# Item 0's tokens by a one-hot product, and layer 0's results summed and normed on token rows

## Chip, cores and metric

One NeuronCore of a Trainium2 chip. The metric is the device time of one execution in microseconds (us). Engines in the profile: PE (TensorE; PEld are its weight loads), DVE (VectorE), ACT (ScalarE), POOL (GpSimd), SP (SyncE, which here only issues transfers). "The granted clock" is the share of TensorE's full clock that the throttle allowed: 1.00 is 2.4 GHz, 0.50 is 1.2 GHz.

## The reference, cut to what matters

288 token rows of width 1024 (256 of a prompt, 8 x 4 of a sample group) pass two layers: a gated chunk MLP and a block-sparse attention, each followed by a mixture of 16 experts.

```python
hp = hp + mixer(rms_norm(hp, norm1[i]))           # i = 0: chunk gating, i = 1: QKV, attention, w_o
hp = hp + hier_moe(rms_norm(hp, norm2[i]), ...)   # the same for the sample rows hs

def hier_moe(h, ...):                             # x: token rows
    g_w, g_idx = top_k(softmax(x @ w_group + b_group), 1)
    e_w, e_idx = top_k(softmax((x @ w_router + b_router)[group g_idx]), 2)
    gates = one_hot(expert, 16) weighted by e_w / sum(e_w) * g_w
    hid = silu(x @ w_gate[e]) * (x @ w_up[e]) * gates[:, e]
    y = sum over e of hid @ w_down[e]
```

All arithmetic on the path of the result is fp32.

## The kernel before

All weights and the cache pages stream from DRAM once. Token rows are worked in three chunks, `tok`: two of 128 rows and one of 32 (the sample). The residual stream lies transposed in `xT` (128 partitions x 8 x 288), the normed input of a product in `hT`. Each engine has one instruction list, in order, and semaphores join them; there is no scheduler, so a wait holds back everything after it on its engine. SP issues nearly all weight transfers, from one queue in program order.

*Into the experts* (`project`, `route`). While the mixer's last product is added to `xT`, PE transposes `xT` back to token rows, six half rows in PSUM banks 0, 1, 2, 3, 4 and 6 (`ROW_ORDER`). ACT squares them, and copies them scaled by the reciprocal root to `tokbuf` and on to DRAM (`h_rows`). DVE ranks the router's logits and gives each token's two choices a slot number, 64 slots to an item (item q < 16 is expert q; experts that get more than 64 tokens have more items at the end).

*Items* (`experts`). For item q, DVE compares each token's slots with 128 lane numbers (`one_hot`, six instructions: three chunks, two choices), PE multiplies the result by `marks` (`table_of`) and DVE sums this to row indices (`indices`). From item 2 on the same table also gives the gate of each slot; items 0 and 1 get theirs in a step of their own (`weigh`, `first_gates`). POOL gathers the 64 token rows, as 128 half rows, from `h_rows`; PE transposes them (`rows_up`, reading columns at a step of four), DVE multiplies by the norm's gain (`x_tile`), PE forms gate and up (`gate_up`), ACT and DVE the gated product, PE transposes it (`gated_up`) and multiplies by the down weights (`down`), ACT copies the result out and POOL scatters it to DRAM (`y_rows`, two results for each token).

The order on PE is: tables 0 and 1, some products that only keep it busy (`idle_products`; in layer 1 the 24 transposes of `rows`, which form token rows of `xT` again for the last sum), gates of items 0 and 1, table 2, `rows_up(0)`, and then for each q: `gate_up(q)`, `gated_up(q-1)`, `table_of(q+3)`, `rows_up(q+1)`, `down(q-1)`.

Expert weights (3 MB an item) go round five buffers: items 0 to 3 are loaded ahead, item 4 (`expert_own`) goes to space that is free only after routing (its down weights to `tokbuf`), and from item 5 on the gate and up weights wait for `gate_up(q-5)`, the down weights for `down(q-5)`.

*Out of layer 0.* SP loads each token's first results into `tokbuf`, ACT the second into `y_second`, chunk by chunk. DVE adds the two, PE transposes to banks 0 to 7, DVE adds to `xT`, ACT squares, PE sums by a product with `mean_d`, ACT takes the root, DVE the reciprocal over 128 x 288 and scales into `hT` (`norm(3)`). Then come 16 QKV tiles of eight products, each tile followed by what normalises and rotates the heads before it. The QKV weights are four quarters of 2 MB.

*Out of layer 1.* The same loads; DVE adds the two results and then the raw rows `x_rows`, chunks in the order 0, 1, sample, and SP stores each.

The lines of the deleted last loop of layer 0 on DVE, and of item 0's start on PE, are in the diff below.

## Time and profile before

| | |
|---|---|
| median of 3 runs | 715.23 us (709.33 to 717.9) |
| the profiled execution | 717.95 us, span 716.1 us |
| mean granted TensorE clock | 0.929 |
| busy: PE, weight loads, DVE, ACT, POOL | 87%, 60%, 38%, 19%, 17% of the span |
| read from DRAM, written | 178.96 MB, 13.50 MB; 269 GB/s over the span |

The profile is of one execution. Busy shares are means over stages with different limits; times in timelines are from the span's start, and a merged row gives the start of its first instruction and the time to the end of its last.

### The profile page before, as it was taken

How to read it: one execution, taken by the hardware profiler on the slowest of the kernel's cores; microseconds unless marked ns; L12 is line 12 of the kernel's file. 1: busy time of each engine (PE TensorE's matmuls, PEld its weight loads, DVE VectorE, ACT ScalarE, POOL GpSimd, SP SyncE). 2: the span in 40 equal slices, each digit the busy share in tenths (PEclk: the TensorE clock that was granted, in tenths of full speed). 3: DMA queues.
4: the chain of work that ended last, by engine and by line, in shares of the span. 5: the costliest groups of instructions: out<-in, count | busy, mean ns of one | idle time of the engine just before them, and what ended most of it. 6: DMA issues, size and time to landing. Idle time of an engine off the chain costs nothing. (4 is left out here: it accounts for less than half of the span.)

```text
span 716.1 us, 11289 instructions
## 1 busy us (share of the span) xinstructions
PE 625.4 (87%) x4125; PEld 427.5 (60%) x4125; DVE 271.6 (38%) x821; ACT 135.2 (19%) x304; POOL 119.1 (17%) x175
## 2 busy tenths in 40 slices
PE   3999999968999988789999997985996899998860
PEld 1777787855655554567667674674785655555430
DVE  2221231144544422435775776340015363442224
ACT  4112001050111111111111454221015211111100
POOL 0000000002232321004222321230000123222110
PEclk9998999977999999789999998998997899999975
DMA  9886004066899993899423765689906789999525
GB/s 342 271 350 234 2 0 184 1 242 239 336 411 409 410 410 158 281 387 339 124 74 111 241 230 185 229 307 392 413 15 247 284 315 411 412 411 413 203 102 199
DMA packets 60980, 184.83 MB, mean 258 GB/s; under 512 B 12244, under 2 KB 12934, under 8 KB 56702
## 3 DMA queue, kind: packets, MB, share of 16 engines
q1 hardware_dynamic: 49022, 153.16, 56.4%
q0 software_dynamic: 10560, 26.24, 10.3%
q10 hardware_dynamic: 1344, 4.72, 1.7%
q8 instruction: 33, 0.54, 0.3%
q14 instruction: 21, 0.17, 0.1%
HBM read 178.96 MB, written 13.50 MB: 269 GB/s over the span
## 5 line engine op out<-in xcount | busy, mean ns | idle before, releaser
L1293 PE MATMUL PS<-hT,half_b 128*128 128x288 f32 x384 | 105.7, 432 | 7.6 <-DMA half_b<-in_b_w_o 4.3
L1293 PEld LDWEIGHTS PS<-hT,half_b 128*128 128x128 f32 x384 | 75.8, 202 | 31.5 <-issue 9.1
L547 POOL DMA_INDIRECT zT<-h_rows,where x35 | 36.2, 1036 | 256.1 <-DMA h_rows<-tokbuf 214.9
L1293 PE MATMUL PS<-hT,half_a 128*128 128x288 f32 x256 | 68.5, 422 | 0.0
L1399 PE MATMUL PS<-ew_in,zT 128*64 128x256 f32 x480 | 58.9, 401 | 4.7 <-DMA ew_in<-in_moe_w_up 3.0
L552 POOL DMA_INDIRECT y_rows<-zT,where x33 | 33.5, 1015 | 159.0 <-ACT zT L708 154.0
L1293 PEld LDWEIGHTS PS<-hT,half_a 128*128 128x128 f32 x256 | 48.7, 195 | 17.7 <-DVE zT L1141 2.8
L1399 PEld LDWEIGHTS PS<-ew_in,zT 128*64 128x64 f32 x480 | 37.9, 146 | 28.4 <-issue 15.9
L1017 DVE COPY zT<-PS 128x128 f32<-128x128 f32 x33 | 9.6, 292 | 110.6 <-PE PS L1410 104.9
L947 DVE TENSOR_SCALAR zT<-lanes,slots 128x128 bf16<-128x128 bf16 (+1 forms) x222 | 39.0, 248 | 2.5 <-DVE slots L1048 1.6
L708 ACT COPY zT<-PS 128x512 f32<-128x512 f32 x33 | 19.3, 586 | 99.5 <-PE PS L1421 99.5
L701 ACT ACTIVATE zT<-PS 64x256 f32<-64x256 f32 x33 | 12.5, 377 | 132.5 <-PE PS L1399 132.5
L857 DVE TENSOR_TENSOR xT<-PS,xT 128x288 f32<-128x288 f32 x16 | 7.3, 458 | 73.9 <-PE PS L1293 73.9
L1005 DVE TENSOR_TENSOR zT<-PS,gains_rows 128x512 f32<-128x512 f32 x35 | 24.2, 691 | 23.0 <-PE PS L1388 22.0
L1293 PE MATMUL PS<-zT,half_a 128*128 128x288 f32 x128 | 32.9, 410 | 0.0
L1421 PE MATMUL PS<-ew_down,zT 128*64 128x512 f32 x120 | 31.4, 647 | 1.3 <-issue 1.3
L1388 PE MATMUL PS<-cst,zT 128*128 128x128 f32 x140 | 27.4, 321 | 2.3 <-DMA zT<-h_rows,where 2.3
L1399 PE MATMUL PS<-sq,zT 128*64 128x256 f32 x96 | 23.5, 401 | 4.5 <-DMA hT<-in_moe_w_up 4.5
L1293 PEld LDWEIGHTS PS<-zT,half_a 128*128 128x128 f32 x128 | 23.7, 190 | 6.1
L1388 PEld LDWEIGHTS PS<-cst,zT 128*128 128x128 f32 x140 | 20.4, 211 | 8.6 <-issue 4.5
L1279 PE MATMUL PS<-cst 128*128 128x288 f32 x64 | 23.9, 538 | 0.0
L1399 PE MATMUL PS<-hT,zT 128*64 128x256 f32 x96 | 23.5, 401 | 0.0
(303 smaller groups left out, 896.0 us busy)
## 6 DMA issues: line engine op xcount, KB each, us to landing
ew_in<-in_moe_w_gate SPq DMA_DIRECT2D x15, 1024.0 KB, 16.2
ew_in<-in_moe_w_up SPq DMA_DIRECT2D x15, 1024.0 KB, 17.9
ew_down<-in_moe_w_down SPq DMA_DIRECT2D x15, 1024.0 KB, 15.8
half_b<-in_moe_w_gate SPq DMA_DIRECT2D x6, 1024.0 KB, 12.9
half_b<-in_moe_w_up SPq DMA_DIRECT2D x6, 1024.0 KB, 15.6
half_b<-in_moe_w_down SPq DMA_DIRECT2D x6, 1024.0 KB, 11.8
half_a<-in_moe_w_gate SPq DMA_DIRECT2D x6, 1024.0 KB, 11.2
half_a<-in_moe_w_up SPq DMA_DIRECT2D x6, 1024.0 KB, 12.8
```

What stands on the lines that cost most here:

```text
L547: pool.indirect_dma_start(out=x_slots[:, u, :], out_offset=None, in_=h_dram.rearrange("t (h n) -> (t h) n", h=2), in_offset=bass.IndirectO ...
L552: pool.indirect_dma_start(out=y_dram[l].rearrange("t k (h n) -> (t k h) n", h=2), out_offset=bass.IndirectOffsetOnAxis(ap=where[:, r, 1:2] ...
L701: act.activation(silu, PS[0:SLOT, 2 + u_of(q), 0:EF], ACT.Silu).then_inc(el["silued"], 1)
L708: act.copy(y_slots[:, u, :], PS[:, 5 + u, :]).then_inc(el["y_sb"], 1)
L947: last = dve.tensor_scalar(hot_of(q)[0:m, c, k, :], lanes[0:m, :], slots[0:m, c, k:k + 1], -float(SLOT * q) if isinstance(q, int) else 0.0 ...
L1005: dve.tensor_tensor(x_slotsT[:, u].rearrange("p j h n -> p (j h) n"), PS[:, u, :].rearrange("p (m n) -> p m n", n=SLOT), gains_rows[:, l, ...
L1017: dve.tensor_copy(hidT, PS[:, 4, 0:FB * SLOT].rearrange("p (f n) -> p f n", f=FB)).then_inc(el["ht_sb"], 1)
L1279: pe.matmul(PS[:, bank, 0:T], ident, cst[:, 0:T], start=True, stop=True)
L1293: mm = pe.matmul(PS[:, bank, 0:T], w[:, k, col:col + P], src[:, k, :], start=(k == 0), stop=(k == KT - 1))
L1388: mm = pe.transpose(PS[:, u, j * P:(j + 1) * P], x_slots[:, u, bass.ds(j, P, 4)], ident)
L1399: mm = pe.matmul(PS[f * SLOT:(f + 1) * SLOT, 2 + u, 0:EF], x_slotsT[:, u, k % 4, k // 4, :], w_in[f][:, k, :], start=(k == 0), stop=(k == ...
L1421: mm = pe.matmul(PS[half * SLOT:(half + 1) * SLOT, 5 + u, :], hidT[:, f, :], w_down[:, f, half * HALF:(half + 1) * HALF], start=(f == 0), ...
```

## The change

Item 0 is no longer gathered. `tokbuf` holds the scaled token rows when they go to DRAM; DVE makes a 0/1 matrix of tokens by the 64 slots of item 0 (`first_hot`), and PE multiplies `tokbuf` (as the weights, columns at a step of four) by it, which gives item 0's tokens transposed in bank 0. For this, in both layers, ACT first copies the six raw half rows from PSUM to `x_rows` (`raw_rows`); in layer 1 this replaces the 24 transposes of `rows`. Table 1 now comes first; table 0, the gates and table 2 come behind `gate_up(0)`. The own expert's down weights wait for the product.

Layer 0's results are summed on token rows with the raw rows, the sample chunk first (`BACK_ORDER`), normed there (ACT's square with a row sum, root, DVE's reciprocal and scaling), and then transposed straight into `hT`. The raw sums are transposed into `xT` between the first four QKV tiles. The second and fourth quarter of the QKV weights are loaded when the sums are done, since the raw rows lie in their space. Layer 1's last sums and stores also take the sample first.

The diff, cut to its core:

```diff
+        hot_first = z_flat[:, 2048:2048 + NT * SLOT].rearrange("p (c n) -> p c n", c=NT)
...
-        Y_ORDER = [KT - 1] + list(range(KT - 1))
+        BACK_ORDER = (CH,) + tuple(range(CH))
...
+                sp.wait_ge(E[l]["xt"], 1)
                 expert_down(l, BUFS - 1, w_down, s_down)
...
-                for c, (at, m) in enumerate(tok):
+                for c in BACK_ORDER:
+                    at, m = tok[c]
...
-            for u in range(4):
+            for u in (0, 2, 1, 3):
+                if u == 1:
+                    sp.wait_ge(S["yt"], NT)
                 load(w_qkv_at[u], w_qkv[:, :, u * HALF:(u + 1) * HALF], s_home[QKV_HOME[u]][0])
...
-                for q in range(2):
-                    pool.wait_ge(E[l]["idx"], 2 * q + 2)
-                    gather(q, q, q)
+                pool.wait_ge(E[l]["idx"], 2)
+                gather(1, 1, 1)
...
+            def raw_rows():
+                for row, half, bank in ROW_ORDER:
+                    n = tok[row][1]
+                    act.copy(x_rows[row][0:n, half * HALF:(half + 1) * HALF], PS[0:n, bank, :]).then_inc(S["xrows_sb"], 1)
...
             route(0)
+            raw_rows()
             experts(0)
-            squares(3)
-            root(3)
-            for i in range(LH + 1):
-                if i < LH:
-                    act.wait_ge(S["qkv_sb"], i + 1)
-                    if i >= KT:
-                        act.wait_ge(S["hms"], i - KT + 1)
-                    act.activation(sq[:, i % KT, :], zT[:, i, :], ACT.Square).then_inc(S["hsq"], 1)
-                if i >= 1:
-                    h = i - 1
-                    act.wait_ge(S["hms"], h + 1)
-                    if h >= 2:
-                        act.wait_ge(S["hrec"], h - 1)
-                    act.activation(std[:, h % 2, :], PS[:, 4 + h % 2, 0:T], ACT.Sqrt, bias=eps[:, :]).then_inc(S["hroot"], 1)
+            ready_for(ACT.Sqrt)
+            for i, c in enumerate(BACK_ORDER):
+                n = tok[c][1]
+                act.wait_ge(S["yt"], i + 1)
+                act.activation(y_squares[0:n, c, :], tokbuf[0:n, c, :], ACT.Square, accum_out=y_sums[0:n, c:c + 1]).then_inc(S["squared"], (3, 3, 2)[i])
+                act.wait_ge(S["squared"], 3 * KT + (3, 6, 8)[i])
+                act.activation(y_std[0:n, c:c + 1], y_sums[0:n, c:c + 1], ACT.Sqrt, bias=eps[0:n, :], scale=1.0 / D).then_inc(S["rooted"], 1)
+            for k in range(KT):
+                act.wait_ge(S["xr_t"], KT + k + 1)
+                act.copy(xT[:, k, :], PS[:, 6 + k % 2, 0:T]).then_inc(S["xr_sb"], 1)
+                if k % 2 == 1:
+                    head_squares(k // 2)
...
+            def first_hot(l):
+                chain.link(dve.scalar_tensor_tensor(out=slot_first[:, :], in0=gates[:, :, 0], scalar=1.0, in1=chosen_any[:, :, 0],
+                                                    op0=ALU.add, op1=ALU.mult))
+                for c, (_, m) in enumerate(tok):
+                    last = dve.tensor_scalar(hot_first[0:m, c, :], lanes[0:m, 0:SLOT], slot_first[0:m, c:c + 1], -1.0,
+                                             ALU.subtract, ALU.is_equal)
+                last.then_inc(S["dispatch"], 1)
...
-                for q in range(2):
-                    one_hot(l, q)
-                    indices(l, q, q)
+                one_hot(l, 1)
+                first_hot(l)
+                indices(l, 1, 1)
                 weigh(l)
+                x_tile(0, 0)
+                one_hot(l, 0)
+                indices(l, 0, 0)
                 first_gates(l)
                 one_hot(l, 2)
                 indices(l, 2, 2)
                 one_hot(l, 3)
...
-            for c, (_, m) in enumerate(tok):
+            def back_sum(i):
+                c, m = BACK_ORDER[i], tok[BACK_ORDER[i]][1]
                 dve.wait_ge(s_yb[c], 2 * 16)
-                dve.tensor_tensor(tokbuf[0:m, c, :], tokbuf[0:m, c, :], y_second[0:m, c, :], ALU.add).then_inc(S["yt"], 1)
-            for i, k in enumerate(Y_ORDER):
-                dve.wait_ge(S["hrows_t"], i + 1)
-                dve.tensor_tensor(xT[:, k, :], PS[:, k, 0:T], xT[:, k, :], ALU.add).then_inc(S["added"], 1)
-            dve.wait_ge(S["added"], KT)
-            norm(3)
+                chain.link(dve.tensor_tensor(tokbuf[0:m, c, :], tokbuf[0:m, c, :], y_second[0:m, c, :], ALU.add))
+                if i == 0:
+                    dve.wait_ge(S["xrows_sb"], 2 * NT)
+                dve.tensor_tensor(tokbuf[0:m, c, :], tokbuf[0:m, c, :], x_rows[c][0:m, :], ALU.add).then_inc(S["yt"], 1)
+            def back_scale(i):
+                c, m = BACK_ORDER[i], tok[BACK_ORDER[i]][1]
+                dve.wait_ge(S["rooted"], 3 + i + 1)
+                dve.wait_ge(S["yt"], i + 1)
+                chain.link(dve.reciprocal(y_rec[0:m, c:c + 1], y_std[0:m, c:c + 1]))
+                dve.tensor_scalar(y_second[0:m, c, :], tokbuf[0:m, c, :], y_rec[0:m, c:c + 1], None, ALU.mult).then_inc(S["x_row"], 1)
+            back_sum(0)
+            back_sum(1)
+            back_scale(0)
+            back_sum(2)
+            back_scale(1)
+            back_scale(2)
+            for k in range(KT):
+                col = KT + k
+                dve.wait_ge(S["hrows_t"], k + 1)
+                dve.tensor_scalar(hT[:, k, :], PS[:, k, 0:T], gains[:, col:col + 1], None, ALU.mult).then_inc(S["normed"], 1)
...
-                for q in range(2):
-                    table_of(q)
-                if l == 1:
-                    pe.wait_ge(S["hrows_sb"], 4 * NT)
-                    rows(xT, "xrows", "xrows_sb", 0)
-                else:
-                    idle_products(4, 5)
-                first_gates()
-                table_of(2)
-                idle_products(3, 5)
-                if l == 1:
-                    pe.wait_ge(S["xrows_sb"], 2 * NT)
-                else:
-                    pe.wait_ge(S["hrows_sb"], 2 * NT)
-                rows_up(0, gathered(0)[1], 0)
+                table_of(1)
+                pe.wait_ge(S["dispatch"], l + 1)
+                pe.wait_ge(S["hrows_sb"], 2 * NT * (l + 1))
+                pe.wait_ge(S["xrows_sb"], 2 * NT * (l + 1))
+                for j in range(4):
+                    for h in range(2):
+                        for c, (_, m) in enumerate(tok):
+                            mm = pe.matmul(PS[:, 0, (2 * j + h) * SLOT:(2 * j + h + 1) * SLOT], tokbuf[0:m, c, bass.ds(h * HALF + j, P, 4)],
+                                           hot_first[0:m, c, :], start=(c == 0), stop=(c == CH))
+                mm.then_inc(el["xt"], 1)
                 for q in range(LAST):
                     gate_up(q, *tiles_in(q), q - 1)
                     if q >= 1:
                         gated_up(q - 1)
+                    else:
+                        table_of(0)
+                        first_gates()
+                        table_of(2)
                     if q + 3 <= LAST + 1:
                         table_of(q + 3)
                     rows_up(q + 1, gathered(q + 1)[1], q)
...
-            for c, (at, n) in enumerate(tok):
-                pe.wait_ge(S["yt"], c + 1)
-                for k in Y_ORDER:
-                    mm = pe.transpose(PS[:, k, at:at + n], tokbuf[0:n, c, k * P:(k + 1) * P], ident[0:n, 0:n])
-                    if c == CH:
+            for i, c in enumerate(BACK_ORDER):
+                at, n = tok[c]
+                pe.wait_ge(S["x_row"], NT + i + 1)
+                for k in range(KT):
+                    mm = pe.transpose(PS[:, k, at:at + n], y_second[0:n, c, k * P:(k + 1) * P], ident[0:n, 0:n])
+                    if i == NT - 1:
                         mm.then_inc(S["hrows_t"], 1)
-            mean_squares(3)
...
+                if i < KT // 2:
+                    for k in (2 * i, 2 * i + 1):
+                        if k >= 2:
+                            pe.wait_ge(S["xr_sb"], KT + k - 1)
+                        for c, (at, n) in enumerate(tok):
+                            mm = pe.transpose(PS[:, 6 + k % 2, at:at + n], tokbuf[0:n, c, k * P:(k + 1) * P], ident[0:n, 0:n])
+                        mm.then_inc(S["xr_t"], 1)
+                if i == KT // 2 - 1:
+                    pe.wait_ge(S["xr_sb"], 2 * KT)
```

## Rows read from the trace of the kernel before

**Rows 1.** The page: busy time by engine, and shares of the chain that ended last.

```profile
PE 625.4 (87%) x4125; PEld 427.5 (60%) x4125; DVE 271.6 (38%) x821; ACT 135.2 (19%) x304; POOL 119.1 (17%) x175
...
PE 10%; DMA 9%; DVE 2%; issue 1%; POOL 0%; ACT 0%; SPq 0%; POOLq 0%; DVEq 0%; ACTq 0%
```

**Rows 2.** Windows of 20 us, experts of layer 0; columns as in the first line.

```profile
core 0: us, PE busy (x) PEld busy (x) DVE busy (x) ACT busy (x) POOL busy (x), PEclk, DMA share, GB/s
200.00:220.00 20.00, 20.00 (x158) 11.73 (x156) 8.01 (x33) 2.89 (x6) 6.05 (x7) 1.00 1.03 410
...
260.00:280.00 20.00, 17.43 (x128) 9.81 (x124) 4.76 (x17) 2.69 (x6) 4.93 (x6) 1.00 0.79 317
```

**Rows 3.** Timeline, entrance to layer 0's experts: start, us, engine, line, operation.

```profile
157.22 0.24 ACT L680 ACTIVATE ex<-ex 128x60 f32<-128x60 f32 x1
...
161.37 1.23 POOL L547 DMA_INDIRECT zT<-h_rows,where  x1 [140.33 <-DMA h_rows<-tokbuf]
...
170.30 5.25 PE L1399 MATMUL PS<-ew_in,zT 128*64 128x256 f32 x32 [0.87 <-DVE zT L1005]
...
177.42 3.67 PE L1399 MATMUL PS<-half_a,zT 128*64 128x256 f32 x32 [0.88 <-DVE zT L1005]
...
184.39 0.34 SPq L378 DMA_DIRECT2D ew_down<-in_moe_w_down  x1
```

**Rows 4.** The same timeline: gates, one_hot(2), table 2, one_hot(3).

```profile
163.40 0.69 PE L1378 MATMUL PS<-marks,zT 128*128 128x3 bf16 x12
...
164.33 1.05 DVE L947 TENSOR_SCALAR zT<-lanes,slots 128x128 bf16<-128x128 bf16 x6
...
165.44 0.39 PE L1367 MATMUL PS<-marks,zT 128*128 128x9 bf16 x6 [1.35 <-DVE zT L947]
...
166.15 1.05 DVE L947 TENSOR_SCALAR zT<-lanes,slots 128x128 bf16<-128x128 bf16 x6
```

**Rows 5.** Timeline, entrance to layer 1's experts.

```profile
549.51 0.24 ACT L680 ACTIVATE ex<-ex 128x60 f32<-128x60 f32 x1
...
551.81 4.77 PE L1352 MATMUL PS<-cst,xT 128*128 128x128 f32 x24
...
552.97 0.59 ACT L687 COPY half_a<-PS 128x512 f32<-128x512 f32 x1 [3.22 <-PE PS L1352]
...
563.36 3.67 PE L1399 MATMUL PS<-ew_in,zT 128*64 128x256 f32 x32 [0.87 <-DVE zT L1005]
...
568.92 3.67 PE L1399 MATMUL PS<-half_a,zT 128*64 128x256 f32 x32 [0.88 <-DVE zT L1005]
```

**Rows 6.** Timeline of PE alone: products with one moving column.

```profile
64.27 4.82 PE L1484 MATMUL PS<-mean_d,sq 128*128 128x1 f32 x48
```

**Rows 7.** Weight loads of two lines: durations in ns, min/median/max.

```profile
L1388 PEld LDWEIGHTS PS<-cst,zT x140: 195/212/231, 168.3 to 695.7; 128*128 128x128 f32 x140
...
L1312 PEld LDWEIGHTS PS<-cst,xT x48: 96/140/144, 132.2 to 540.7; 128*128 128x128 f32 x32, 128*32 128x32 f32 x16
```

**Rows 8.** Windows of 1 us, columns as in rows 2.

```profile
166.00:167.00 1.00, 1.00 (x5) 0.70 (x5) 0.97 (x8) 0.00 (x0) 0.00 (x0) 0.85 1.02 418
...
173.00:174.00 1.00, 1.00 (x10) 0.71 (x8) 0.00 (x0) 0.00 (x0) 0.00 (x0) 0.74 0.00 0
```

**Rows 9.** Timeline, layer 0's results to the first QKV tile.

```profile
294.67 1.23 DVE L1131 TENSOR_TENSOR tokbuf<-tokbuf,zT 128x1024 f32<-128x1024 f32 x1 [4.69 <-DMA zT<-y_rows]
...
297.96 2.35 DVE L1131 TENSOR_TENSOR tokbuf<-tokbuf,zT 128x1024 f32<-128x1024 f32 x2 [2.06 <-DMA zT<-y_rows]
...
312.14 9.69 PE L1293 MATMUL PS<-hT,half_b 128*128 128x288 f32 x32 [3.29 <-DVE hT L850]
```

**Rows 10.** Timelines of ACT, DVE and PE: row square, row scaling, three transposes.

```profile
8.62 1.04 ACT L735 ACTIVATE zT<-tokbuf 32x1024 f32<-32x1024 f32 x1
...
10.54 1.40 DVE L1078 TENSOR_SCALAR zT<-tokbuf,rec 128x1024 f32<-128x1024 f32 x2
...
43.69 0.56 PE L1526 MATMUL PS<-cst,tokbuf 128*128 128x128 f32 x3
```

**Rows 11.** Timeline, layer 1's last sums.

```profile
708.87 1.22 DVE L1270 TENSOR_TENSOR tokbuf<-tokbuf,zT 128x1024 f32<-128x1024 f32 x1 [1.20 <-DMA tokbuf<-y_rows]
```

More of the change, by code:

```diff
@@ L306, in gathered, with turn_of @@
         def gathered(q):
-            return f"in{q % 2}", 16 * (q // 2 + 1)
+            return f"in{q % 2}", 16 * ((q + 1) // 2)
+        def turn_of(q):
+            return 1 - q if isinstance(q, int) and q < 2 else q
         def scattered(q):
@@ L680, in route @@
                 act.activation(ex[:, :, :], ex[:, :, :], ACT.Exp).then_inc(S["exped"], 1)
-            def rows(src_sem, base, dst, done):
-                for i in range(2 * NT):
-                    _, n = tok[i // 2]
-                    act.wait_ge(S[src_sem], base + i + 1)
-                    act.copy(dst[i // 2][0:n, (i % 2) * HALF:(i % 2 + 1) * HALF], PS[0:n, i % 4, :]).then_inc(S[done], 1)
+            def raw_rows():
+                for row, half, bank in ROW_ORDER:
+                    n = tok[row][1]
+                    act.copy(x_rows[row][0:n, half * HALF:(half + 1) * HALF], PS[0:n, bank, :]).then_inc(S["xrows_sb"], 1)
             def experts(l):
@@ L836, in _ @@
             route(1)
-            rows("xrows", 0, x_rows, "xrows_sb")
+            raw_rows()
             experts(1)
@@ L1263, in _ @@
             past_rows(1)
+            dve.wait_ge(S["xr_sb"], 2 * KT)
             project(KT)
@@ L1343, in route @@
                 idle_products(3, 5)
-            def rows(src, s, taken, base):
-                for i in range(2 * NT):
-                    at, n = tok[i // 2]
-                    if i >= 4:
-                        pe.wait_ge(S[taken], base + i - 3)
-                    for j in range(4):
-                        mm = pe.transpose(PS[0:n, i % 4, j * P:(j + 1) * P], src[:, (i % 2) * 4 + j, at:at + n], ident)
-                    mm.then_inc(S[s], 1)
             def experts(l):
```

50 lines of the change are left out of this document (33 added, 17 removed).

## Prediction, made before the change was run

> **What bounds the kernel now.** Read the page first: TensorE (PE) is busy for 87% of a 716.1 us span, and the chain that ended last is made of PE and DMA pieces in nearly equal parts [rows 1]. So a saving counts only where PE or a transfer stands still for it, and the next view must be one by stage. The 20 us windows show the expert stage: PE busy 20.00 of 20 while the DMA engines are at 1.03 of their share, 410 GB/s, until a stretch before 280 in which PE has waits again [rows 2]. PE and weight transfers are in step through the stage, and a delay at its entrance is handed on to its exit. The reason is SP's queue: the down weights of item 5 are issued at 184.39, when item 0's down product has ended, and all later weights stand behind them [rows 3]. From there the transfers are back to back. Whatever moves 184.39 moves the end of the stage.
>
> Third view: the timeline of the entrance to layer 0's experts. ACT finishes the exponent at 157.46; the gather of item 0 starts at 161.37, when the rows written to DRAM have landed; item 0's gate/up product starts at 170.30 and takes 5.25 us (item 1's takes 3.67), item 1's starts at 177.42 [rows 3]. Between the two lies a gap of only 1.9 us (170.30 + 5.25 to 177.42) for one table, four transposes and their scaling. Layer 1 has the same shape: exponent done at 549.75, product 0 at 563.36, product 1 at 568.92 [rows 5]. Last, the two tails: layer 0's from the landed results to the first QKV tile, 297.96 to 312.14 [rows 9], and layer 1's from its second landed chunk, 708.87, on [rows 11].
>
> **Part 1, item 0 by a product (both layers).** Removed: one gather and four transposes in each layer, and in layer 1 the 24 transposes of the raw rows, 4.77 us of PE [rows 5]. Added in front of product 0: four small vector instructions (DVE is through them before ACT is, so nothing on the path), six ACT copies, and the product itself. The copies are a new wait: the product waits for all six raw row halves, and behind it in PE's queue is the whole expert stage. In layer 0 ACT starts them at 157.46; the copy of a 128x512 bank takes 0.59 us [rows 5], six take 3.5, so PE may begin at 161.0. In layer 1: 549.75 + 3.5 = 553.25.
>
> The product is 24 fp32 matmuls, recorded as 48 instructions, each with a 128-column weight load and 64 moving columns. Nothing in the trace has that form. The nearest below: 48 instructions with one moving column took 4.82 us, 0.10 us each [rows 6]. The nearest above: 24 transposes took 4.77 us, 0.20 us each, most of them at the half clock [rows 5]. The weights here are read from tokbuf with a step of four elements. Loads with that step (L1388) take 195 ns at least, those without (L1312) 96 to 144, so some 0.05 to 0.1 us more each, part of it hidden [rows 7]. I take 0.14 us an instruction at the full clock and 0.22 at half. While ACT copies, PE has one small table to do, so the product begins at half, and product 0 in layer 0 shows what that costs: 5.25 against 3.67, 1.6 us, so 3.2 us were run at half speed [rows 3], with the granted clock at 0.74 in the window at 173, where it came back [rows 8]. So 3.4 us at half do 15 instructions, 33 more take 4.6: 8.0 us, between 4.8 (all full, no stride) and 10.6 (all half). Gate/up 0 follows after the scaling, and then, its clock being up, takes 3.65. The scaling I put at 0.86 with its hand-overs: the present gap of 1.9 us is a table (0.3 beyond product 0), transposes (0.75) and this. End of gate/up 0: 161.0 + 8.0 + 0.86 + 3.65 = 173.5, two microseconds before the 175.55 of now.
>
> A page of the Trainium skill bears on that step: "SBUF — State Buffer", section "Door 1: The DMA port swizzle", says that lines are 16 bytes and that a stride is free up to four fp32. By it the product would go at 0.10 and 0.20 us an instruction, 6.5 us, and the whole change would come out 3 us lower; the rows of L1388 and L1312 [rows 7] speak against a free step of four, and they decide.
>
> Next, what is put between product 0 and product 1. PE's order there becomes table 0, the gates, table 2, table 3, the transposes of item 1, and each waits for DVE and DVE for it, so it is one chain: table 0 with two index steps on DVE 0.75, gates with their sum 1.1, one_hot(2) 1.05, table 2 with index steps 0.75, one_hot(3) 1.05, table 3 0.45, transposes 0.75, scaling 0.86. The durations are those of the same instructions where they stand now: gates 0.69, one_hot 1.05, a table 0.39, and from the start of a table at 165.44 to the next one_hot at 166.15 0.71 [rows 4]. The sum is 6.7 us, where 1.9 stands today: +4.8 in each layer, uncovered, since PE is in order and item 1's gate/up is behind it. Now these instructions run while the gather is on its way; that cover is what the change gives up.
>
> In those 6.7 us PE does little. The trace has such a gap: after small table products the granted clock fell between 166 and 167 [rows 8]. So I add 1.6 us, the price that product 0 pays today, to product 1. Sum for layer 0: product 1 starts at 173.5 + 6.7 = 180.2 instead of 177.42, plus 1.6 of clock: +4.4. Layer 1: 553.25 + 8.0 + 0.86 + 3.65 + 6.7 + 1.6 - 568.92 = +5.1. Bounds: with a product of 4.8 us and no fall of the clock -0.4 and +0.3; with 10.6 and 2.5 us of clock +7.9 and +8.6. Of the queues: SP now holds the own expert's down half (item 4) until the product has ended; behind it stands item 5, which waits for the end of gate/up 0 anyway, so nothing. POOL issues one gather fewer; item 2's now comes out some 3.8 us after the end of gate/up 0, beside 2 MB of weights, and is wanted 11 us after it: nothing, and if it lands later than that, its lateness.
>
> **Part 2, layer 0's results on token rows.** Now: second chunk landed at 297.96, then sums, transposes, additions, squares, mean products, a 288-column reciprocal, scaling, QKV at 312.14 [rows 9]. After: the sample chunk comes first, between issue and the 294.67 of the first whole chunk, and delays the last one by its 256 KB, a quarter of the 3.3 us between whole chunks [rows 9], 0.8: 298.8. On it: two sums of 1.22 us [rows 11], a square of 1.04 and a scaling of 0.70 [rows 10], a root, a reciprocal and their hand-overs (an estimate, 0.7), the first transposes and one scaling into hT (an estimate, 1.1). That is 298.8 + 2.45 + 1.04 + 0.70 + 0.7 + 1.1 = 304.8, 7.4 us sooner. The transposes of the first two chunks hide under this. DVE may do the sample's scaling between the sums, so 5 to 8.
>
> It is paid back in part. The raw rows are transposed for xT between QKV tiles, where PE has no idle time. Three such transposes take 0.56 us with their tail, some 0.40 without [rows 10], so eight of them are 3.2 us, and the wait for ACT's last two copies is some 0.65: -7.4 + 3.85 = -3.5 us, bounds -1 and -5. The second and fourth quarter of the QKV weights are issued only after the sums, near 301.4, but the results and two other quarters before them in the queue are 6 MB, which at the 410 GB/s of [rows 2] last until 306 or later, and the second quarter is wanted four tiles after the first: nothing; were it late, each 2 MB is 5 us. What stands behind them in SP's queue, the key pages, is used after all QKV tiles.
>
> **Part 3, order of the last sums.** DVE now does four sums after the second chunk has landed, 4.9 us at 1.22 [rows 11]. With the sample's two done early, two remain, 2.45; the chunk lands some 0.6 later, and the last store carries 512 KB, not 128, perhaps 0.4 more: -1.5, bounds -0.5 and -2.5.
>
> **Sum.** +4.4 + 5.1 - 3.5 - 1.5 = +4.5 us. The profiled execution took 717.95 us (span 716.1), so it would take 722.5. The median of the runs shown is 715.23, 2.7 lower; on it, 719.7.
>
> **Rivals.** (a) The clock stays up: the product at 5.5 us, no fall in the gap. Then +0.3 and +1.0 in front, and -5 behind: -3.7, about 711.5. For it: gate/up in layer 1 ran at 3.67 us throughout [rows 5]. Against: the fall in [rows 8], behind work of just this kind. (b) The entrance doesn't count, because the weights, not PE, set the stage's end: then only the tails remain, -5, about 710. For it: the DMA engines are full in [rows 2]. Against: the weight queue starts on item 0's down product [rows 3]. (c) Slower: the product runs wholly at half clock, 10.6 us, and product 0 behind it too. This decides once PE stands nearly still while ACT copies, as it does here, and the product itself is too thin to bring the clock back. Then 2.6 + 1.6 more in each layer, 8.4 over my sum, about 728. (d) The gain of part 2 fails, QKV running at half clock from its start while the raw rows cost more: then +8, about 723; it lies inside my range.
>
> **How the numbers follow.** The forecast, with (d) inside, 55%; (a) 20%, (b) 13%, (c) 12%. The range reaches from just below (b), 709, to (c), 728; the runs before spread from 709 to 718 by themselves. What a measurement here can tell from no change is about 2%, 14 us. A gain of that size is beyond all lower bounds together (-0.4 + 0.3 - 5 - 2.5 = -7.6), so 2%; a loss of that size only at the far end of (c), 6%; within, 92%.
>
> **What would show it.** In the profile after: the product's start about 161 and 553 and its length near 8 us; 6.7 us from the end of gate/up 0 to the start of gate/up 1, with a clock of 0.5 in it; item 5's down weights issued some 4 us later than now; QKV some 7 us nearer to the landed results, then four sets of six transposes between tiles; two sums, not four, after the last landing. I am wrong if the tables run beside gate/up 0, if the product takes under 6 us, or if the clock holds through the gap.

## The result, and the profile after

The changed kernel took 740.37 us (median of 4 runs, 738.37 to 741.0) against 712.56 for the kernel before (4 runs, 709.33 to 717.9): ratio 1.0362, 95% interval 1.031 to 1.0414. It is slower by 3.6%, outside the range of 709 to 728. The profiled execution took 738.37 us, span 736.7, mean granted clock 0.912 against 0.929.

Layer 0's entrance in the timeline of the changed kernel, which answers to [rows 3, 4] (the same steps under other line numbers):

```profile
160.21 14.28 PE L1487 MATMUL PS<-zT,tokbuf 128*128 128x64 f32 x48 [2.71 <-ACT half_b L709]
...
175.37 5.82 PE L1446 MATMUL PS<-ew_in,zT 128*64 128x256 f32 x32 [0.87 <-DVE zT L1039]
...
182.05 0.69 PE L1425 MATMUL PS<-marks,zT 128*128 128x3 bf16 x12 [0.54 <-DVE where L993]
...
184.09 0.39 PE L1414 MATMUL PS<-marks,zT 128*128 128x9 bf16 x6 [1.35 <-DVE zT L981]
...
185.96 0.39 PE L1414 MATMUL PS<-marks,zT 128*128 128x9 bf16 x6 [1.48 <-DVE zT L981]
...
188.17 6.24 PE L1446 MATMUL PS<-half_a,zT 128*64 128x256 f32 x32 [0.88 <-DVE zT L1039]
...
197.70 0.34 SPq L384 DMA_DIRECT2D ew_down<-in_moe_w_down  x1
```

The product starts when the sixth copy is done and takes 14.28 us; gate/up 0 and 1 take 5.82 and 6.24 us, where they took 5.25 and 3.67 before [rows 3]. Windows of the same stretch, columns as in [rows 8]:

```profile
155.00:160.00 5.00, 2.51 (x11) 1.47 (x10) 4.32 (x25) 4.59 (x10) 0.00 (x0) 0.50 0.80 302
...
161.00:165.00 4.00, 4.00 (x15) 3.41 (x14) 0.00 (x0) 0.57 (x2) 0.98 (x1) 0.50 0.99 351
165.00:170.00 5.00, 5.00 (x18) 4.42 (x18) 0.00 (x0) 0.00 (x0) 0.00 (x0) 0.50 0.40 162
170.00:174.00 4.00, 4.00 (x15) 3.41 (x15) 0.00 (x0) 0.00 (x0) 0.00 (x0) 0.50 0.00 0
```

From 161 to 174, inside the product, PE is busy in every microsecond, and weight loads are under way for 11.24 of these 13 us. The granted clock stays at 0.50 from before the product to its end. Layer 1 repeats it (compare [rows 5]); the first line is the exponent, a mark of the table below:

```profile
559.49 0.24 ACT L703 ACTIVATE ex<-ex 128x60 f32<-128x60 f32 x1
...
562.71 14.28 PE L1487 MATMUL PS<-zT,tokbuf 128*128 128x64 f32 x48 [2.68 <-ACT half_b L709]
577.87 5.96 PE L1446 MATMUL PS<-ew_in,zT 128*64 128x256 f32 x32 [0.87 <-DVE zT L1039]
...
600.47 0.34 SPq L384 DMA_DIRECT2D ew_down<-in_moe_w_down  x1
```

Both tails of the changed kernel, which answer to [rows 9, 11]:

```profile
303.20 1.29 SPq L384 DMA_DIRECT2D tokbuf<-y_rows  x3
...
309.07 1.22 DVE L1169 TENSOR_TENSOR tokbuf<-tokbuf,zT 128x1024 f32<-128x1024 f32 x1 [0.16 <-DMA zT<-y_rows]
...
319.17 4.32 PE L1350 MATMUL PS<-hT,half_b 128*128 128x288 f32 x16
...
719.84 1.52 SPq L384 DMA_DIRECT2D tokbuf<-y_rows  x3
...
728.74 1.23 DVE L1327 TENSOR_TENSOR tokbuf<-tokbuf,zT 128x1024 f32<-128x1024 f32 x1 [3.35 <-DMA tokbuf<-y_rows]
...
731.14 1.22 DVE L1327 TENSOR_TENSOR tokbuf<-tokbuf,zT 128x1024 f32<-128x1024 f32 x1
```

And the milestones of the kernel before that no row above gave: loads of layer 0's results, layer 1's item 5, layer 1's last item (gate/up, down), loads of layer 1's results.

```profile
289.37 1.29 SPq L378 DMA_DIRECT2D tokbuf<-y_rows  x3
...
575.88 0.34 SPq L378 DMA_DIRECT2D ew_down<-in_moe_w_down  x1
...
683.28 6.45 PE L1399 MATMUL PS<-ew_in,zT 128*64 128x256 f32 x32 [2.98 <-DMA ew_in<-in_moe_w_up]
691.97 3.34 PE L1421 MATMUL PS<-ew_down,zT 128*64 128x512 f32 x8 [0.43 <-issue]
699.56 1.50 SPq L378 DMA_DIRECT2D tokbuf<-y_rows  x3
```

| stretch, in the two profiles | predicted | measured |
|---|---|---|
| layer 0, to item 5's down weights (184.39, 197.70) | +4.4 | +13.3 |
| from there to the loads of the results (289.37, 303.20) | 0 | +0.5 |
| from there to layer 1's exponent (549.51, 559.49) | -3.5 | -3.9 |
| from there to item 5's down weights (575.88, 600.47) | +5.1 | +14.6 |
| from there to the loads of the results (699.56, 719.84) | 0 | -4.3 |
| from there to the end of the span (716.1, 736.7) | -1.5 | +0.3 |

The sum is +20.6. The medians differ by 27.8; the 7.2 us between lie in which run was profiled: before's, 717.95, was the slowest of its four, the changed kernel's, 738.37, the fastest. The loss is made at the two entrances. What was open: why an instruction of the product takes 0.30 us (14.28 / 48), whether the step of four in its weight loads, the half clock or the narrow moving side; and what each other part is worth.

### The profile page after: what moved, and what is told of

Same layout as the page of the kernel before. It is cut to its first block and busy times, and to the rows that moved or that the text cites. A ratio compares the mean times of both kernels' runs of the same rounds, so it can differ in the third digit from the quotient of the medians.

```text
span 736.7 us, 11418 instructions
## 1 busy us (share of the span) xinstructions
PE 639.9 (87%) x4177; PEld 441.7 (60%) x4177; DVE 274.2 (37%) x829; ACT 141.2 (19%) x318; POOL 116.7 (16%) x173
## 5 line engine op out<-in xcount | busy, mean ns | idle before, releaser
L1350 PE MATMUL PS<-hT,half_b 128*128 128x288 f32 x384 | 103.8, 426 | 4.3 <-DMA half_b<-in_b_w_o 4.3
L1350 PEld LDWEIGHTS PS<-hT,half_b 128*128 128x128 f32 x384 | 74.7, 199 | 26.9 <-issue 5.6
L557 POOL DMA_INDIRECT zT<-h_rows,where x33 | 34.1, 1033 | 280.8 <-DMA h_rows<-tokbuf 214.2
L1446 PE MATMUL PS<-ew_in,zT 128*64 128x256 f32 x480 | 60.5, 409 | 4.7 <-DMA ew_in<-in_moe_w_up 2.9
L1487 PE MATMUL PS<-zT,tokbuf 128*128 128x64 f32 (+1 forms) x96 | 28.6, 457 | 5.4 <-ACT half_b L709 5.4
L1487 PEld LDWEIGHTS PS<-zT,tokbuf 128*128 128x128 f32 (+1 forms) x96 | 24.7, 321 | 9.0 <-issue 5.5
L1446 PE MATMUL PS<-half_a,zT 128*64 128x256 f32 x192 | 27.0, 445 | 1.8 <-DVE zT L1039 1.8
L1350 PEld LDWEIGHTS PS<-zT,half_a 128*128 128x128 f32 x128 | 23.7, 190 | 6.1
L1435 PE MATMUL PS<-cst,zT 128*128 128x128 f32 x132 | 25.6, 319 | 1.8 <-DMA zT<-h_rows,where 1.8
L1446 PE MATMUL PS<-sq,zT 128*64 128x256 f32 x96 | 21.8, 380 | 3.3 <-DMA hT<-in_moe_w_up 3.3
```

The costliest lines, as they stand in the source:

```text
L557: pool.indirect_dma_start(out=x_slots[:, u, :], out_offset=None, in_=h_dram.rearrange("t (h n) -> (t h) n", h=2), in_offset=bass.IndirectO ...
L1350: mm = pe.matmul(PS[:, bank, 0:T], w[:, k, col:col + P], src[:, k, :], start=(k == 0), stop=(k == KT - 1))
L1435: mm = pe.transpose(PS[:, u, j * P:(j + 1) * P], x_slots[:, u, bass.ds(j, P, 4)], ident)
L1446: mm = pe.matmul(PS[f * SLOT:(f + 1) * SLOT, 2 + u, 0:EF], x_slotsT[:, u, k % 4, k // 4, :], w_in[f][:, k, :], start=(k == 0), stop=(k == ...
L1487: mm = pe.matmul(PS[:, 0, (2 * j + h) * SLOT:(2 * j + h + 1) * SLOT], tokbuf[0:m, c, bass.ds(h * HALF + j, P, 4)], hot_first[0:m, c, :], s ...
```

## The experiments

Each stands against the changed kernel unless it says otherwise; ratios are to the kernel before, measured beside each run. Runs 2 to 6 and 10 are one execution each and are read from their profiles. "The exponent" is ACT's `ex` row, with which an entrance begins; "the results' loads" are SP's loads of `y_rows`, with which it and the items end.

**1. The tails alone.** Item 0 gathered as before, tails as changed (ACT's six copies stay, and in layer 1 idle products stand where 24 transposes stood before):

```diff
-                table_of(1)
...
-                mm.then_inc(el["xt"], 1)
+                for q in range(2):
+                    table_of(q)
+                idle_products(4, 5)
+                first_gates()
+                table_of(2)
+                idle_products(3, 5)
...
+                rows_up(0, gathered(0)[1], 0)
```

> Item 0 is gathered again, with the idle products and the order of small steps of the kernel before, in both layers; the two tails stay as changed. The theory that the whole loss is made at the two entrances to the experts: they go back to their old times (item 5's down weights issued near 184.4, second layer likewise), and the time is that of the kernel before less the 3.9 us that layer 0's tail gained, plus 0.3 for layer 1's: some 3.6 us less than before, ratio 0.995. The rival, that the tails cost by themselves what the pair of traces hides (6 MB in another order, the raw rows between tiles): the time is at or above that of before. A second rival, that the medians differ by 28 us where the traces differ by 21, so 7 us lie elsewhere: then this kernel stands 3 us or more above before.

Measured: 710.0 us (10 runs) against 714.58 (13 runs), ratio 0.9932, interval 0.9892 to 0.9973. From the loads of layer 0's results to layer 1's exponent it takes 256.0 us, as in the changed kernel (256.3) and 4.1 less than before (260.1):

```profile
286.36 1.29 SPq L384 DMA_DIRECT2D tokbuf<-y_rows  x3
...
542.36 0.24 ACT L703 ACTIVATE ex<-ex 128x60 f32<-128x60 f32 x1
```

From the exponent to item 5's down weights it takes 25.6 and 26.9 us in the two layers, near the 27.2 and 26.4 of before; in the changed kernel it takes 40.7 and 41.0. The loss is in the entrances; layer 0's tail is a gain by itself.

**2. No step.** ACT writes `tokbuf` with its columns in the order (half, j, p), and the weight loads of the product, and of the items' four transposes, read a run of 128. The product's weights (the lines are cut to them):

```diff
...
-  tokbuf[0:m, c, bass.ds(h * HALF + j, P, 4)]
+  tokbuf[0:m, c, h * HALF + j * P:h * HALF + (j + 1) * P]
...
```

> The changed kernel, only that ACT writes the scaled rows with their columns in the order in which the product and the transposes read them, so that no weight load steps over four elements. Theory of the step: the product's 0.30 us an instruction is the load with a step at half clock, and without it an instruction takes the 0.20 us of the transposes without a step at half clock: the product falls from 14.28 to about 9.6 us in each layer, item 5's down weights come near 193 instead of 197.7, the whole some 9 us shorter. Theory of the clock: the step hides and the half clock alone makes 0.30; the product stays at 14.3 us, the time within 1 us of the changed kernel's. In both gate/up 0 stays near 5.8.

Measured: product 13.32 us in both layers, 738.57 us. At half clock the step costs 0.02 us an instruction. The theory of the step fell, as it was put. The total says little of the step: ACT's two writes of a chunk now take 2.04 us instead of 1.27, so that the exponent comes 2.3 us later (159.32 against 156.98), and from there to item 5's down weights it takes 1.9 us less (2.2 in layer 1).

The items' transposes show the step's price at the full clock. Their weight loads between 200 and 260, where the granted clock was 1.00, in the changed kernel and in this run (durations in ns, min/median/max):

```profile
L1435 PEld LDWEIGHTS PS<-cst,zT x36: 194/212/221, 201.7 to 256.4; 128*128 128x128 f32 x36
```

```profile
L1435 PEld LDWEIGHTS PS<-cst,zT x36: 138/140/143, 202.2 to 256.2; 128*128 128x128 f32 x36
```

**3. A full clock ahead of the product**, by eight idle products after table 1:

```diff
                 table_of(1)
+                idle_products(8, 5)
```

> The changed kernel with eight idle products of 288 columns (results unused) on TensorE between the first table and the product, in both layers. They begin near 157.5 while ACT copies and, half of them at half clock, end near 163.5, 3 us later than the product's start now. Theory of the clock: the product then begins at full clock and takes 0.15 us an instruction, 7.1 us, and gate/up 0 behind it 3.7: start of product 163.5, end 170.6, gate/up 0 over at 175.2 against 181.2, so 6 us a layer shorter. Theory of the step: at full clock a load with a step still takes its 0.195 to 0.23 us, so the product takes 9.6 to 10. Theory of the thin product: the clock falls again during the product, which then takes 10 to 12 us with a granted clock between 0.5 and 1, and gate/up 0 runs at half again (5.8).

Measured: 744.4 us; product 13.88 and 13.85 us, gate/up 0 6.43 and 5.17. The product began at full clock, and lost it with PE busy throughout. Two windows of this run:

```profile
163.00:164.00 1.00, 1.00 (x5) 0.93 (x5) 0.00 (x0) 0.00 (x0) 0.00 (x0) 1.00 0.99 406
...
165.00:166.00 1.00, 1.00 (x5) 0.88 (x4) 0.00 (x0) 0.00 (x0) 0.00 (x0) 0.50 1.02 414
```

The thin product drops the clock; that theory held. But at the full clock 12 instructions still took 3.20 us, 0.27 each (the expectation of run 4 misreads this as 0.20). So the clock alone buys little either.

**4. Both at once**, the edits of 2 and 3:

> The run with eight idle products, and with the scaled rows written so that no weight load steps over four elements (both edits at once). In the run with the idle products alone the product began at full clock, did 0.20 us an instruction until the granted clock fell 3 to 4 us later, and took 13.88 us. Theory that the step costs as much time at full clock as at half (0.02 us an instruction, the difference between the product with and without it at half clock): 0.18 us an instruction while the clock is up, product 13 us. Rival, that the step is what made 0.20 of the 0.14 that was predicted: 0.10 to 0.14 us an instruction at full clock, so 25 to 35 instructions are through before the clock falls, product 9 to 11 us. In both the clock falls in the product. If it holds, its fall in the other run came from the step's slow loads: product 6.7 to 8.6, gate/up 0 at 3.67.

Measured: 732.88 us; product 10.67 and 10.44 us. The product's weight loads in run 3 and in this one, each while the clock was up and after it fell (durations in ns, min/median/max); first the run with the step:

```profile
L1488 PEld LDWEIGHTS PS<-zT,tokbuf x12: 303/325/329, 161.0 to 164.0; 128*128 128x128 f32 x8, 32*128 32x128 f32 x4
...
L1488 PEld LDWEIGHTS PS<-zT,tokbuf x22: 304/326/329, 165.7 to 171.9; 128*128 128x128 f32 x15, 32*128 32x128 f32 x7
```

without it:

```profile
L1488 PEld LDWEIGHTS PS<-zT,tokbuf x20: 181/188/193, 162.5 to 165.4; 128*128 128x128 f32 x14, 32*128 32x128 f32 x6
...
L1488 PEld LDWEIGHTS PS<-zT,tokbuf x22: 283/333/334, 166.9 to 172.7; 128*128 128x128 f32 x14, 32*128 32x128 f32 x8
```

Here a load with the step of four takes 325 ns at either clock; one without takes 188 at full and 333 at half. So the two faults cover for each other: at half clock removing the step hardly shows, at full clock the step takes back most of what the clock gives, and only both edits together bring an instruction down, to 0.16 us (21 in 3.36 us). Then too the clock falls inside the product (1.00 in the window at 165, 0.51 at 166), so the slow loads with the step are not what drops it. Of the theories put down for this run the first, 13 us, fell; the rival's 9 to 11 us came true, at 0.16 us an instruction and not at 0.10 to 0.14.

The Trainium skill, "SBUF — State Buffer", section "Door 1: The DMA port swizzle", has a step of up to four fp32 free. For these loads, 325 against 188 ns at full clock, and for the transposes' of run 2, 212 against 140, the trace disagrees.

**5. The small steps inside the product.** Table 0, gates and table 2 between its quarters, item 0's scaling behind one_hot(3):

```diff
+                    if j == 0:
+                        table_of(0)
+                    if j == 1:
+                        first_gates()
+                    if j == 2:
+                        table_of(2)
```

> The changed kernel; only table 0, the gates and table 2 are put between the quarters of item 0's product, and item 0's scaling behind one_hot(3), so that table 3, item 1's transposes and the scaling alone are left between gate/up 0 and gate/up 1. Theory that the chain of small steps is a loss by itself, beside the product's: the product with the tables in it takes some 15.8 us, the gap falls from 6.98 to about 1.9 us, and with no gap behind gate/up 0, which brings the clock back, gate/up 1 takes 3.7 instead of 6.24: 6 us less in each layer, about 726 in all. Rival, that the small steps were not the limit (the scaling or item 1's rows are late anyway): the gap stays over 4 us and the time within 3 us of the changed kernel's.

Measured: 724.54 us, against 726 expected. In layer 1:

```profile
573.28 5.13 PE L1446 MATMUL PS<-ew_in,zT 128*64 128x256 f32 x32 [0.87 <-DVE zT L1039]
580.28 3.67 PE L1446 MATMUL PS<-half_a,zT 128*64 128x256 f32 x32 [0.87 <-DVE zT L1039]
```

The gap is 1.9 us (573.28 + 5.13 to 580.28) instead of 7.1, and gate/up 1 keeps the clock that gate/up 0 brought back. The chain of small steps was worth its 5 us a layer, and its clock 2.5 more. With what the product now takes longer, exponent to item 5's down weights is 6.9 and 7.2 us shorter.

**6. The operands changed over.** The one-hot matrix as weights, the token rows moving, then a copy and four transposes:

```diff
+  pe.matmul(PS[h * SLOT:(h + 1) * SLOT, 1, :], hot_first[0:m, c, :],
+            tokbuf[0:m, c, h * HALF:(h + 1) * HALF], start=(c == 0), stop=(c == CH))
```

> Item 0 still by a one-hot product, with the operands' parts changed: the one-hot matrix (64 columns) is the weight, and the token rows move past it, 512 columns at a time, in 6 matmuls (12 instructions); VectorE copies the 128 gathered rows out of PSUM and TensorE transposes them as a gathered item's. At half clock an instruction of 512 columns takes at least 0.43 us, so 12 take 5.1 us or more if 512 columns cost as gate/up's 256 do twice over (0.182 us for 256 at half), 5 at the least; copy 0.7, transposes 1.1: 7.0 instead of 14.28. If the wide product brings the clock back as gate/up does, gate/up 0 takes 3.7 to 5. Theory that the form of the product is what failed: item 5's down weights near 189 to 190 instead of 197.7, the whole 12 to 15 us below the changed kernel. Rival, that any product in fp32 costs the same for the same arithmetic: 14 us again, and 2 us more for copy and transposes.

Measured: 725.87 us; in layer 0, at half clock throughout, the product takes 5.58 us for the same arithmetic, 12 instructions of 512 columns. Layer 0, with gate/up 0 behind it, and layer 1's product:

```profile
160.28 5.58 PE L1488 MATMUL PS<-tokbuf,zT 128*64 128x512 f32 x12 [2.71 <-ACT half_b L709]
...
168.66 5.85 PE L1448 MATMUL PS<-ew_in,zT 128*64 128x256 f32 x32 [0.87 <-DVE zT L1039]
...
556.11 4.26 PE L1488 MATMUL PS<-tokbuf,zT 128*64 128x512 f32 x12 [2.68 <-ACT half_b L709]
```

The form failed, not the idea. Twice as many columns pass (12 x 512 against 48 x 64), so it was not they that made 14.28 us, which leaves the 48 weight loads, of which 12 with half the columns are left (between 162 and 166 they are under way for 0.56 of 4 us). The hope that the wide product brings the clock back came true in one layer only: in layer 0 it does not, and gate/up 0 takes 5.85; in layer 1 the clock is at 1.00 in the window at 559, inside the product, which takes 4.26, and falls again at 562 (0.61), where PE waits behind it, and gate/up 0 takes 5.06. The Trainium skill, "TensorEngine Tiling (Array Packing)", section "When to Use Tiling", names this exchange for a moving side of 64 columns or fewer, together with column tiling; 14.28 against 5.58 us agrees with the exchange; what column tiling adds to it no run here shows.

**7. The same with a full clock, small steps first.** Idle products around table 0 while ACT copies; gates and table 2 ahead of gate/up 0:

```diff
                 table_of(1)
+                idle_products(3, 5)
+                table_of(0)
+                idle_products(3, 5)
```

> Item 0 by the product with the one-hot matrix as weights and the token rows moving, as in the run with rows moving; now with six idle products around table 0 while ACT copies, so that TensorE doesn't stand still before it, and the gates and table 2 ahead of gate/up 0. Theory that the form and the clock are the two faults, and the idea itself good: product from 160.3 at full clock, 12 instructions at 0.22, 2.6 us; copy, transposes, small steps 3 us; gate/up 0 from 166, 3.7 us; gate/up 1 from 171.6, against 175.6 in the kernel with the tails alone; item 5's down weights near 178.5 against 182.6. About 4 us a layer below that kernel, 8 in all, ratio 0.98 against the kernel before. Rival, that the clock falls in the product again as it did behind the eight idle products: product 5.6, gate/up 0 from 169 at 5.8, item 5's down weights at 185 or later, ratio 1.0 or above. Second rival, that the entrance gains but the stage behind hands nothing on, its transfers setting the end: item 5's down weights earlier and layer 0's results loaded at the same time as with the tails alone, ratio 0.993.

Measured: 702.9 us (4 runs), ratio 0.9873, interval 0.9805 to 0.994, to the kernel before.

```profile
161.95 2.94 PE L1491 MATMUL PS<-tokbuf,zT 128*64 128x512 f32 x12
...
167.56 3.67 PE L1448 MATMUL PS<-ew_in,zT 128*64 128x256 f32 x32 [0.29 <-DVE zT L1039]
...
180.08 0.34 SPq L384 DMA_DIRECT2D ew_down<-in_moe_w_down  x1
```

The clock holds from 160 on, both gate/ups take 3.67 in both layers, and item 5's down weights are 2.5 us ahead of run 1 (182.57), which arrives at the results' loads (283.92 against 286.36). Exponent to item 5's down weights takes 23.1 and 23.3 us: the two entrances are worth 6.1 us against run 1. The start is 1.65 us later than expected: the second three idle products outlast the copies.

**8. Fewer idle products,** against run 7. None after table 0, and the store of the sample's output behind the two stores of whole chunks instead of ahead of them:

```diff
                 table_of(0)
-                idle_products(3, 5)
...
-            sp.dma_start(o["ys"].rearrange("b t d -> (b t) d"), tokbuf[0:TSA, CH, :]).then_inc(S["y_out"], 16)
             for c in range(CH):
...
+            sp.dma_start(o["ys"].rearrange("b t d -> (b t) d"), tokbuf[0:TSA, CH, :]).then_inc(S["y_out"], 16)
```

> The kernel with rows moving and idle products, without the three idle products behind table 0, and with the store of the sample's output behind the two stores of whole chunks. At the entrances: the product can begin at 160.4 instead of 161.95 and at 545.8 instead of 547.4. Theory that the three idle products before table 0 are what brings the clock back and the rest only costs their time: gate/up 0 1.5 us earlier in each layer, both at 3.67, 3 us in all. Rival, that the product falls at half clock without them: it takes 5.6 us and gate/up 0 4 to 5.9, so 1 us or more is lost in each layer. At the end: theory that the sample's store, issued 5.7 us after the loads, holds up the first whole chunk's landing: it lands 5.2 to 5.9 us after the issue of the loads (8.1 to 9.75 in the three runs with the sample first so far), and issue to end falls from 16.0 to about 14.5. Rival, that the loads themselves land together: 8 to 9.8 again, and issue to end 16 to 17.7.

and with one after table 0, the store where it was:

> The kernel with rows moving and idle products, with one idle product instead of three behind table 0; the end as changed, the sample's store first. Both theories of the run with none: product from 160.95 and 546.3, 1 us earlier in each layer than with three, if the clock holds; ratio some 2 us under that kernel's 0.987. If the clock falls: gate/up 0 slower, ratio 0.99. At the end, with the sample's store first: first whole chunk 8 to 9.8 us after the issue of its load, issue to end 16 to 17.7.

Measured: 707.36 us (5 runs; 0.9921, 0.9891 to 0.995) and 706.44 (6 runs; 0.9907, 0.988 to 0.9933). With none:

```profile
159.40 2.94 PE L1489 MATMUL PS<-tokbuf,zT 128*64 128x512 f32 x12 [0.24 <-ACT half_b L708]
...
165.33 5.03 PE L1447 MATMUL PS<-ew_in,zT 128*64 128x256 f32 x32 [0.29 <-DVE zT L1038]
```

and its windows:

```profile
163.00:164.00 1.00, 0.98 (x10) 0.74 (x10) 0.75 (x5) 0.00 (x0) 0.00 (x0) 1.00 1.06 434
...
165.00:166.00 1.00, 0.71 (x6) 0.54 (x6) 0.97 (x7) 0.00 (x0) 0.00 (x0) 0.50 1.05 422
```

The product runs at full clock, as the theory said, but the clock is lost in the small steps behind it, which neither theory had: gate/up 0 takes 5.03 and 5.29 us in the two layers (5.11 and 5.21 with one). What is saved ahead is lost behind: exponent to item 5's down weights takes 23.0 and 23.9 us with none, 23.4 and 23.7 with one, 23.1 and 23.3 with three. The 4 us between the totals lie for the most part elsewhere, in layer 1's items: from item 5's down weights to the results' loads it takes 123.2 and 123.0 us here, 119.4 in run 7. The last item alone takes 9.8 us in gate/up and down here (6.21 + 3.59 and 6.29 + 3.51) and 7.3 in run 7 (5.36 + 1.94). Whether the entrance has to do with that stays open.

**9. The old order at the end** (layer 1's last loads, sums and stores), on the kernel of run 1 and on that of run 7. The sums:

```diff
-            for c in BACK_ORDER:      # sample, 0, 1
+            for c in range(NT):       # 0, 1, sample
```

> The kernel with the tails alone, with layer 1's last loads, sums and stores in the order of the kernel before (chunks 0, 1, sample). Theory that sample first delays the first whole chunk by more than the two sums that it saves (it landed 9.75 us after the issue of its load there, 5.63 in the kernel before): from the issue of the results' loads to the end 16.6 us instead of 17.7, ratio 0.3 to 1 us below that kernel's, 0.992. Rival, that the late chunk has nothing to do with the order (a transfer behind it, chance): 17 to 18 us from issue to end again, or more, the ratio 0.995.

> The kernel with rows moving and three idle products on either side of table 0, with layer 1's last loads, sums and stores in the order of the kernel before. Theory that both entrances are 2.5 to 4 us shorter than with a gathered item 0, and that the order at the end is worth nothing: item 5's down weights near 180, gate/up 0 at 3.67 in both layers, first whole chunk 5.2 to 5.7 us after the issue of its load, issue to end 16.1 to 16.8, ratio 0.985 to 0.99 and below that of the two kernels with the tails alone (0.993 and 0.995). Rival, that the 702.9 us of the first run of this entrance were luck, the clock falling ahead of gate/up 0 in other runs as it did with fewer idle products: ratio 0.992 or above.

Measured: 710.42 us (10 runs; 0.9946, 0.9899 to 0.9994) and 702.73 (6 runs; 0.9874, 0.9833 to 0.9915). The second repeats run 7's 702.9, with gate/up 0 at 3.67 us in both layers, so that time was not luck. The first whole chunk's sum, here in the last kernel and then in the kernel of run 1, whose loads were issued at 684.03 and 691.72:

```profile
689.68 1.23 DVE L1329 TENSOR_TENSOR tokbuf<-tokbuf,zT 128x1024 f32<-128x1024 f32 x1 [5.42 <-DMA zT<-y_rows]
```

```profile
701.47 1.23 DVE L1325 TENSOR_TENSOR tokbuf<-tokbuf,zT 128x1024 f32<-128x1024 f32 x1 [4.03 <-DMA tokbuf<-y_rows]
```

It starts 5.2 to 5.7 us after the issue in the four profiles with the sample last, 6.7 to 10.2 in the ten with it first (8.0 or more in nine), with its store last too (9.5, run 8): the store is not the cause. From the issue of these loads to the end of the span it takes 16.1 to 16.8 us (mean 16.5) with the sample last and 14.8 to 18.2 (mean 16.8) with it first. The order shows no gain.

**10. The kernel before again:**

> The kernel before once more, for a second profile. In the first one gate/up 0 of layer 0 ran partly at half clock (5.25 us), with the tails alone it took 3.67 there and 5.35 in layer 1. Theory that the clock's return near gate/up 0 falls now on one side, now on the other, and that the 7 us by which the two medians differ more than the two profiles are such luck in the profiled run of before: this profile differs from the first by 1.5 us or more at layer 0's or layer 1's entrance, and nowhere else by as much. Rival, that the profile's spread is elsewhere, in the attention or in the transfers: both entrances agree within 0.5 us with the first and other stages differ.

Measured: 717.38 us, span 715.6. Gate/up 0 takes 3.67 us instead of 5.25 and item 5's down weights come at 182.27 instead of 184.39, as the theory said; but the stage behind takes 2.4 us longer and the results' loads are at 289.66 (289.37). So neither theory held whole: the entrance does vary with the clock, and the stage behind it varies as much, from 103.8 to 107.4 us over all profiles.

## Why the prediction was wrong, point by point

**The product's term failed**, 8.0 us with an upper bound of 10.6, measured 14.28. Start and number of instructions were right (160.21 for 161.0; 48). At half clock I took 0.22 us an instruction from the transposes of [rows 5]; it is 0.30. At full clock I took 0.10 from [rows 6] and some 0.04 for the step; it is 0.16 without and 0.27 with the step. [Rows 7] had shown the step's price, 195 ns against 96 to 144, and I called part of it hidden; here loads take 325 against 188 ns and are under way for 11.24 of 13 us, so little of it is. The bounds were no bounds, since both came from other forms.

**The clock's return failed with it.** I had the product bring the clock back after 3.4 us, a figure that no run shows for it (gate/up 0 of [rows 3] had run 3.2 us at half clock); it does not bring the clock back in its 14.28 us, and loses it where it had it (runs 3 and 4). A row that I used had shown this: in the product of [rows 6], 64.27 to 69.09, with one moving column and PE busy throughout, the clock fell as well:

```profile
66.00:67.00 1.00, 1.00 (x11) 1.00 (x11) 0.00 (x0) 0.00 (x0) 0.00 (x0) 1.00 1.01 414
...
68.00:69.00 1.00, 1.00 (x17) 0.98 (x17) 0.00 (x0) 0.00 (x0) 0.00 (x0) 0.50 1.02 418
```

So gate/up 0 took 5.82, not 3.65, and gate/up 1 2.6 us of clock, not 1.6. This was rival (c), at 12%, with its place and its condition right and its price for the product, 10.6 us, too low.

Layer 0's entrance then closes by its terms, measured less predicted: start -0.8, product +6.3, gate/up 0 +2.2, gap +0.3, gate/up 1 +1.0: 9.0 over +4.4, 13.4, measured 13.3. Layer 1 by the same terms: -0.5, +6.3, +2.3, +0.4, +1.0: 9.5 over +5.1, measured 14.6.

**Right:** the chain of small steps (6.7 us, though its terms add up to 6.76; 6.98 and 7.1; shown by run 5); that item 5's weights hand the delay on (in layer 0 13.3 became 13.8, in layer 1 14.6 became 10.3), against rival (b); that the clock falls in the gap, against rival (a); layer 0's tail, -3.5 (-3.9; run 1), where the first QKV tile starts 6.8 us sooner after the issue of the results' loads (I said 7.4), with four sets of transposes between tiles.

**Layer 1's tail, -1.5, failed:** +0.3, and by run 9 the order is worth nothing. I had two sums left after the last landing. There are mostly four, since the first whole chunk then lands about when the second does: in the changed kernel its first sum starts at 728.74, and the second chunk's, at 731.14, waits for nothing. Where it came early, 6.7 us after the issue in run 4, the tail took 14.8 us, 1.7 less than before, near the gain I had put down; that is one profile. Why it is late elsewhere is open: in layer 0, with the same order of loads, it came 5.9 us after the issue.

In layer 1, 4.3 us came back in the stage, where I had put nothing. From item 5's down weights to the results' loads the profiles take 119.0 to 124.2 us, 119.0 to 123.2 of them with a changed entrance, so that any of it is due to the change is not shown. Of the 4.3, 2.7 are its last item, which runs at one clock or the other: gate/up 6.45 and down 3.34 us before, here in the changed kernel:

```profile
705.82 5.14 PE L1446 MATMUL PS<-ew_in,zT 128*64 128x256 f32 x32 [2.91 <-DMA ew_in<-in_moe_w_up]
713.62 1.94 PE L1468 MATMUL PS<-ew_down,zT 128*64 128x512 f32 x8 [0.43 <-issue]
```

## What to carry to other kernels

A product with a narrow moving side is priced by its weight loads: put the narrow operand on the weights' side (14.28 to 5.58 us at half clock), and see what the wide product and the steps around it do to the granted clock (2.94 us at the full clock, and 3.67 for gate/up 0 behind it). When an edit that removes a suspected cost changes nothing, try it again with the other suspect gone: step and clock each hid the other, and only with both gone did the product's instructions come down (0.30 to 0.16 us). A bound from a neighbouring row holds only if that row has the same form on both operands; and look up in the windows what the row's own product did to the clock.

## What had not been expected of the hardware

A busy PE can lose its clock: with PE busy in every microsecond of the thin product the grant went from 1.00 to 0.50 (runs 3 and 4), as in a product with one moving column before (64.27 to 69.09). In this product a weight load of 128 fp32 columns with a step of four took 325 ns at both clocks, one without 188 at full and 333 at half; in the items' transposes, at the full clock, 212 and 140 (run 2). Idle products whose time looked wasted kept 3.67 us for gate/up 0 (runs 7 and 9) where 5.0 to 5.3 stood with fewer (run 8).
